# Gate rows of a routed expert layer: a table layout with two tokens side by side, and the low parts of 24 weight blocks moved from GpSimd to VectorE

## The reference

```
q = (xb @ w_q).reshape(T, 8, 2, 128)
s = einsum('thpd,hpkd->thpk', q, sub_keys)
sv, si = top_k(s, 16)
cand = sv[:, :, 0, :, None] + sv[:, :, 1, None, :]
top_s, pos = top_k(cand, 16)
eidx = 128 * si0[pos] + si1[pos]
gate = softmax(top_s)
act = gelu(einsum('thkd,td->thk', expert_u[eidx], xb))
out = einsum('thk,thkd->td', gate * act, expert_v[eidx])
```

## Time and profile before

| what | value |
|---|---|
| median of 3 runs | 3770.73 us (3764.57 to 3774.24) |
| the profiled execution, own time | 3768.24 us |
| its span, first to last instruction | 3766.5 us |
| PE busy | 3357.8 us (89% of the span) |
| DVE busy | 2283.6 us (61%) |
| ACT busy | 1297.5 us (34%) |
| POOL busy | 781.2 us (21%) |
| gate stage, first line 960 matmul to the first matmul behind the last batch | 2232.51 to 2545.09 us |

### The profile page before, as it was taken

How to read it: one execution, slowest core, us unless ns; L and a number is a source line. 1 busy time by engine, 2 the same in 40 slices (tenths; PEclk the granted TensorE clock), 3 DMA queues, 4 the chain that set the end, 5 groups by cost and what they waited for, 6 DMA issues and landing times. The chain is left out here.

```text
span 3766.5 us, 40330 instructions
## 1 busy us (share of the span) xinstructions
PE 3357.8 (89%) x16396; PEld 2605.7 (69%) x16396; DVE 2283.6 (61%) x3542; ACT 1297.5 (34%) x1837; POOL 781.2 (21%) x512
## 2 busy tenths in 40 slices
PE   5678888889879799888898889997999999999997
PEld 2456666667657566666676669986888888888874
DVE  4667777776466965545588777764665444444444
ACT  4233333333332245422322235552322322222222
POOL 0344444344122211000001221211222111111100
PEclk8888889889988899999999889998999999999998
DMA  4111111112411111122223325546654333333330
GB/s 156 45 54 59 59 62 57 62 54 87 154 64 56 56 45 40 40 84 79 78 73 112 101 88 167 174 148 224 201 191 156 124 123 118 122 118 118 118 122 28
DMA packets 164808, 378.33 MB, mean 100 GB/s; under 512 B 10640, under 2 KB 77072, under 8 KB 164496
## 3 DMA queue, kind: packets, MB, share of 16 engines
q1 hardware_dynamic: 164624, 375.76, 29.9%
HBM read 318.04 MB, written 57.67 MB: 100 GB/s over the span
## 5 line engine op out<-in xcount | busy, mean ns | idle before, releaser
L556 PE MATMUL ps<-hT,wsp 128*128 128x512 f32 x2120 | 890.7, 420 | 157.2 <-POOL wsp L2161 44.6
L557 PE MATMUL ps<-hT,wsp 128*128 128x512 f32 x2120 | 849.8, 401 | 0.0
L558 PE MATMUL ps<-hT,wsp 128*128 128x512 f32 x2120 | 848.8, 400 | 0.0
L556 PEld LDWEIGHTS ps<-hT,wsp 128*128 128x128 f32 x2120 | 414.2, 195 | 278.3 <-issue 157.2
L2161 POOL TENSOR_TENSOR wsp<-ring,wsp 128x1024 fp32r<-128x1024 f32 x153 | 380.5, 2490 | 882.3 <-ACT wsp L1020 882.0
L558 PEld LDWEIGHTS ps<-hT,wsp 128*128 128x128 f32 x2120 | 412.1, 194 | 91.5
L557 PEld LDWEIGHTS ps<-hT,wsp 128*128 128x128 f32 x2120 | 415.1, 196 | 83.3 <-issue 5.7
L1020 ACT ACTIVATE wsp<-ring 128x1024 fp32r<-128x1024 f32 x355 | 367.6, 1052 | 145.7 <-PE ps L558 120.3
L2270 POOL TENSOR_TENSOR ex<-ex 128x512 fp32r<-128x512 f32 x128 | 175.2, 1383 | 933.4 <-ACT ex L1379 933.4
L2114 DVE TENSOR_TENSOR xT<-ps,xT 128x512 f32<-128x512 f32 x256 | 175.3, 689 | 287.9 <-PE ps L558 287.9
L1424 DVE TENSOR_TENSOR wsp<-ring,wsp 128x1024 fp32r<-128x1024 f32 x202 | 253.6, 1257 | 157.2 <-ACT wsp L1020 156.9
(11 more groups left out here) (371 smaller groups left out, 4885.7 us busy)
## 6 DMA issues: line engine op xcount, KB each, us to landing
ring<-in_eu SPq DMA_DIRECT2D x128, 512.0 KB, 3.3
ring<-in_ev SPq DMA_DIRECT2D x128, 512.0 KB, 3.6
gd<-oh SPq DMA_DIRECT2D x8, 4096.0 KB, 14.6
ex<-gd SPq DMA_DIRECT2D x32, 1024.0 KB, 6.6
ring<-in_ein SPq DMA_DIRECT2D x57, 512.0 KB, 3.2
ring<-in_ada SPq DMA_DIRECT2D x48, 512.0 KB, 3.2
ring<-in_oin SPq DMA_DIRECT2D x40, 512.0 KB, 3.2
ex<-zd SPq DMA_DIRECT2D x15, 1024.0 KB, 8.9
```

What stands on the lines that cost most here:

```text
L556: pe.matmul(out, W[0], R[0], start=first, stop=False)
L557: pe.matmul(out, W[0], R[1], start=False, stop=False)
L558: return pe.matmul(out, W[1], R[0], start=False, stop=last)
```

## The change

`QT` becomes 2, so that PE's step is 2 elements, that is 4 bytes. To keep DVE's runs at 4 elements, each table `ixT` is written twice over: for every pair of tokens (a, b) it holds a b a b, and DVE handles two values of n and two tokens as one run of four. The tables take 1024 instead of 512 elements per partition, their space is found by letting the gate stage's first gelu tile be `gT`, and the set `on_pool` loses blocks 32 to 55, so DVE makes those low parts.

```
-QT = 4
+QT = 2
...
-        ixT = [ar0(512, BF16) for _ in range(5)]
+        ixT = [ar0(1024, BF16) for _ in range(5)]
...
-        xo = [a(512) for _ in range(2)]
+        xo = [gT, a(512)]
...
-        on_pool |= {n for n, (name, u) in enumerate(UNITS) if name == "eu" and 32 <= u < 56}
...
-        def quads(ap):
+        def pairs(ap):
             return ap.rearrange("p (o n t) -> p o n t", n=128, t=QT)
+        def twice(ap):
+            return ap.rearrange("p (o r t) -> p o r t", r=2, t=QT)
+        def again(ap):
+            return ap.rearrange("p (o r t) -> p o r t", r=1, t=QT).broadcast_to([128, ap.shape[1] // QT, 2, QT])
...
                     for q in range(4):
+                        tk = t4 * 4 + q
                         for m in range(3):
-                            r = pe.matmul(out[:, q * 128:(q + 1) * 128], quads(o[0])[:, t4, :, q], quads(o[1 + m])[:, t4, :, q],
+                            r = pe.matmul(out[:, q * 128:(q + 1) * 128], pairs(o[0])[:, tk // QT, :, tk % QT], pairs(o[1 + m])[:, tk // QT, :, tk % QT],
...
-                for i, o in enumerate((ixT[0], ixT[1], gT)):
-                    act.activation(o[:, blk * 128:(blk + 1) * 128], all_b.at["ij", blk][:, i * 128:(i + 1) * 128],
-                                   ACT.Copy).then_inc(scalar_done, A.step("ij", blk))
+                for i in range(2):
+                    act.activation(twice(ixT[i][:, blk * 256:(blk + 1) * 256]),
+                                   again(all_b.at["ij", blk][:, i * 128:(i + 1) * 128]), ACT.Copy).then_inc(
+                        scalar_done, A.step())
+                act.activation(gT[:, blk * 128:(blk + 1) * 128], all_b.at["ij", blk][:, 256:384], ACT.Copy).then_inc(
+                    scalar_done, A.step("ij", blk))
...
-                    dve.tensor_copy(ixT[2], gT).then_inc(vector_done, V.step())
+                    dve.tensor_copy(twice(ixT[2]), again(gT)).then_inc(vector_done, V.step())
...
-                return ixT[i][:, t0:t0 + TB].rearrange("p (o n t) -> p o n t", n=1, t=QT).broadcast_to(
-                    [128, TB // QT, 128, QT])
+                return ixT[i][:, 2 * t0:2 * (t0 + TB)].rearrange("p (o n t) -> p o n t", n=1, t=2 * QT).broadcast_to(
+                    [128, TB // QT, 64, 2 * QT])
+            def by_two(ap):
+                return ap.rearrange("p (o n t) -> p o n t", n=64, t=2 * QT)
...
-                keys_ = iom.rearrange("p (o n t) -> p o n t", o=1, t=QT).broadcast_to([128, TB // QT, 128, QT])
-                dve.tensor_tensor(quads(oi), keys_, spread_(0, t0), ALU.is_equal).then_inc(vector_done, V.step())
+                keys_ = by_two(iom).broadcast_to([128, TB // QT, 64, 2 * QT])
+                dve.tensor_tensor(by_two(oi), keys_, spread_(0, t0), ALU.is_equal).then_inc(vector_done, V.step())
```

More of the change, by code:

```diff
@@ L2064, in soft @@
                     w.wait_ge(scalar_done, A("ij", 3))
-                    dve.tensor_copy(ixT[2], gT).then_inc(vector_done, V.step())
+                    by_t = lambda ap: ap.rearrange("p (o t) -> p o t", t=QT)
+                    dve.tensor_copy(twice(ixT[2]), again(gT)).then_inc(vector_done, V.step())
                     own()
-                    dve.tensor_tensor(rT0, gT, ixT[2], ALU.subtract).then_inc(vector_done, V.step())
+                    dve.tensor_tensor(by_t(rT0), by_t(gT), twice(ixT[2])[:, :, 0, :], ALU.subtract).then_inc(
+                        vector_done, V.step())
                     own()
-                    dve.tensor_copy(ixT[3], rT0).then_inc(vector_done, V.step())
+                    dve.tensor_copy(twice(ixT[3]), again(rT0)).then_inc(vector_done, V.step())
                     own()
-                    dve.tensor_tensor(rT0, rT0, ixT[3], ALU.subtract).then_inc(vector_done, V.step())
+                    dve.tensor_tensor(by_t(rT0), by_t(rT0), twice(ixT[3])[:, :, 0, :], ALU.subtract).then_inc(
+                        vector_done, V.step())
                     own()
-                    dve.tensor_copy(ixT[4], rT0).then_inc(vector_done, V.step("split"))
+                    dve.tensor_copy(twice(ixT[4]), again(rT0)).then_inc(vector_done, V.step("split"))
             def spread_(i, t0):
-                return ixT[i][:, t0:t0 + TB].rearrange("p (o n t) -> p o n t", n=1, t=QT).broadcast_to(
-                    [128, TB // QT, 128, QT])
+                return ixT[i][:, 2 * t0:2 * (t0 + TB)].rearrange("p (o n t) -> p o n t", n=1, t=2 * QT).broadcast_to(
+                    [128, TB // QT, 64, 2 * QT])
+            def by_two(ap):
+                return ap.rearrange("p (o n t) -> p o n t", n=64, t=2 * QT)
             def hot(tb):
@@ L2085, in hot @@
                 w.wait_ge(iom_in, 16)
-                keys_ = iom.rearrange("p (o n t) -> p o n t", o=1, t=QT).broadcast_to([128, TB // QT, 128, QT])
-                dve.tensor_tensor(quads(oi), keys_, spread_(0, t0), ALU.is_equal).then_inc(vector_done, V.step())
+                keys_ = by_two(iom).broadcast_to([128, TB // QT, 64, 2 * QT])
+                dve.tensor_tensor(by_two(oi), keys_, spread_(0, t0), ALU.is_equal).then_inc(vector_done, V.step())
                 w.wait_ge(vector_done, V.was("hot", tb - 1))
-                dve.tensor_tensor(quads(oj), keys_, spread_(1, t0), ALU.is_equal).then_inc(vector_done, V.step())
+                dve.tensor_tensor(by_two(oj), keys_, spread_(1, t0), ALU.is_equal).then_inc(vector_done, V.step())
                 own()
                 for g, i in ((g1, 2), (g2, 3), (g3, 4)):
-                    dve.tensor_tensor(quads(g), quads(oj), spread_(i, t0), ALU.mult).then_inc(vector_done, V.step("hot", tb))
+                    dve.tensor_tensor(by_two(g), by_two(oj), spread_(i, t0), ALU.mult).then_inc(vector_done, V.step("hot", tb))
             def z(c, j, n):
```

## The result

The changed kernel takes 3816.47 us (median of 4 runs, 3814.91 to 3821.41) against 3767.65 us for the kernel before in the same comparison (four runs; the table ahead has three of them). The ratio is 1.0131, 95% interval 1.0111 to 1.0150: **slower by 1.3%**, 49 us. The forecast was 3830 us, range 3797 to 3860. The profiled execution took 3816.89 us, 48.65 more than that of before.

What follows compares the result with a forecast made beforehand. The wait of DVE's low part for ACT's high part was to set the pace: 23 x 13.9, 8 x 5.80 and 6.0 make 372.1 us, +59.5; in all +61.3, so 3830 us, range 3797 to 3860.

Steps and rivals of the forecast that it cites:

- The chain: Gate stage: copies, ACT's high part, DVE's low part, one-hots, next batch in sequence; 12.72 us a step at full clock.
- rival 2: Line 968's matmuls stay at 117 ns despite the new layout: +86 us, 3854 us; chance 0.23.
- an exception in the old trace (batch 30): In the old gate stage DVE, not POOL, made the low part before batch 30; that step took 14.93 us, not 11.15.
- The steps without a block: 8 of the stage's 31 steps have neither block nor low part; DVE's five instructions set their pace, 5.80 us each.
- The matmul: Gate stage's 128-column matmuls fall from 117 ns to 64 to 67 ns at full clock, lower end taken.
- The clock: PE's idle stretches of about 4 us make its clock fall; with 25 slow matmuls a block step takes 13.9 us.
- The tail: From batch 31's start to the first matmul behind the stage: 4.8 to 7.0 us, taken as 6.0.
- The casts: Ahead of the stage, three casts write 1024 elements instead of 512: 0 to +2.4 us, taken as +2.0.
- the clock did not hold: A rival claimed PE's clock holds through the stage's idle stretches: +33 us, 3801 us; chance 0.15.
- the faster case: A rival claimed the low part does not hold the one-hots and stage steps are PE's: 3690 us; chance 0.07.
- The 4.0 us within which a low part has to start: Limit from a batch's start for the faster case; rows show 7.84 us, 5.63 the least worked out.
- Costed at nothing: Low parts of blocks 32 and 33, SP's load starts and DVE instructions longer than 1.22 us: no cost assumed.

Runs made afterwards that it cites:

- e2: The kernel before with only the low parts moved to DVE, tokens four to a group as before: 3846.94 us, ratio 1.0211.
- e1: The changed kernel with the low parts of blocks 32 to 55 given back to POOL, two-token layout kept: 3698.85 us, ratio 0.9812.
- e3: The changed kernel with DVE's low parts issued behind the batch's one-hots instead of in front of them: 3688.24 us, ratio 0.9788.
- e5: The changed kernel with ACT making the high part one block earlier, low parts still in front of the one-hots: 3674.94 us, ratio 0.9747.
- e8: e3 with the tables written once, so DVE's inner run is 2 elements instead of 4: 3683.51 us, ratio 0.9779.
- e9: The changed kernel with low parts behind the one-hots, high part one block earlier and tables written once: 3673.50 us, ratio 0.9750.
- e4: The changed kernel with 12 extra, thrown-away matmuls of 512 columns in front of each of the 24 woven blocks: 3805.81 us, ratio 1.0104.
- e7: The kernel before, four tokens to a group, with low parts on DVE behind the one-hots: 3762.94 us, ratio 0.9989.

## Why the prediction was right, by its steps

- **The chain** held within 0.03 us where the clock was full: high part, low part and next batch forecast at 4.54, 5.63 and 12.72 us, measured 4.51, 5.62 and 12.70. So close a match is partly luck: the first copy came 0.09 us sooner than forecast (0.90 for 0.99), and from there to the high part it took 0.06 longer (3.61 for 3.55). e2 gave the forecast of rival 2's stage (397 us) without a fitted number. That an exception in the old trace (batch 30) would become the rule was the step on which all rests, and e1, e3 and e5 each confirm it by another edit.
- **The steps without a block**: 5.80 us as forecast.
- **The matmul**: taken as 64 ns at full clock, measured 57. The 11 ns over 53 that I carried from the 512-column matmuls were too many. By the cacheline rule of the Trainium skill ("Advanced Engine Details and Errata", SBUF Cachelines) 8 bytes should already have been free; 117 against 57 ns decide against it for these operands.
- **The clock**: the fall came as forecast, but not in every step, and this is the term that was mis-sized. The forecast gave all 23 steps with a block 25 slow matmuls. In 7 of them the batch ran at full clock, and the step was 12.68 to 12.70 us: the first of the stage, and six behind the second of two batches without a block between. The other 16 took 13.30 to 14.41 us, 13.79 on average. PE's timeline has one of either kind, 12.68 and 14.41 us:

```profile
2264.07 2.93 PE L968 MATMUL ps<-oh 128*128 128x128 bf16 x48 [1.30 <-DVE oh L2109]
...
2276.75 5.30 PE L968 MATMUL ps<-oh 128*128 128x128 bf16 x48 [4.21 <-DVE oh L2109]
...
2291.16 4.22 PE L968 MATMUL ps<-oh 128*128 128x128 bf16 x48 [3.45 <-DVE oh L2109]
```

That the slow steps came so near to 13.9 is partly luck. Their matmuls were priced at 117 ns, the old layout's pace, and took 107, which by the same chain makes 13.6 us of a step with 25 slow ones; but in some batches there were more of these, 48 of 48 in the one at 2276.75. The forecast of the stage was 11.6 us too high (372.1 for 360.5): 7 x 1.2 = 8.5 for the batches at full clock, 16 x 0.11 = 1.8 for the others, and the tail.

- **The tail**: 6.0 forecast, 2592.22 - (2581.69 + 5.80) = 4.7 measured, 1.3 us.
- **The casts**: +2.0 taken, 3 x 0.26 = +0.8 measured (0.69 against 0.43 us).
- **Rivals**: the clock did not hold; the matmuls did become faster; the faster case is what comes once the low part does not wait: e5 takes the wait away and comes to 3675 us, where 3690 was worked out. Most of the 15 us between them is the matmul again, 8 x 4 x (3.1 - 2.74) = 11.5. The 4.0 us within which a low part has to start so that the change is no loss were not tried.
- **Costed at nothing**, and rightly: the low parts of blocks 32 and 33 (behind the second of them DVE still waits 0.45 us for the constant), SP's loads (no engine waits for one in the stage), the one-hots' length (1.22 us each).

What stays open is when exactly the clock falls. Of the eight batches that come second in a pair, seven ran at full clock, with PE idle for 1.3 to 1.7 us ahead of them, and the one at 2310.26, with 2.88 us, did not; no run varies this by itself. Only one execution of the changed kernel has a trace, but its four runs lie within 7 us and their mean clocks within 0.926 to 0.930.

## What to carry to other kernels

When work moves to another engine, look at what the moved instruction waits for and what stands behind it there, not only at the busy times: DVE had the time, and a low part of 1.2 us cost 13.45 - 8.29 = 5 us each time because its input came late. Look in the old trace for the one place where the new order already exists; here batch 30 showed every link of the chain that the change made the rule. And a part that looks like a loss can hide a gain beside it: each half of this change had to be run alone to see +79 us and -70 us, and their sum, +9, is not what they cost together.

## What the runs showed of the hardware

- A bfloat16 matmul of 128 columns whose operands step by 8 bytes took 117 ns at a granted clock of 1.00 (the kernel before) and of 0.50 (e2) alike. With a step of 4 bytes it took 57 ns and 107 ns (the changed kernel). Which of its two operands, weights or moving, sets the 117 was not tried.
- VectorE kept 1.22 us for 2048 bfloat16 elements with broadcast runs of two elements (4 bytes; e8, e9) as with runs of four.
- 12 extra matmuls of 512 columns per block, thrown away, made the gate stage 12 us shorter (e4: 348.3 for 360.5), as they kept the clock at 0.96 to 1.00 instead of 0.84 to 0.91 in a stage that waits for others.
- A GpSimd low part stretched a VectorE comparison beside it from 1.22 to 3.42 us (e1), and three products from 3.50 to 5.57 (the kernel before). With the slow matmul, doing without it gave next to nothing beyond batch 30's step (e7: 5 us, 4 of them that step). With the fast one e3 is 10.6 us below e1; 4.4 of these are batch 30's step again, and the rest was not taken apart.
